# Cross attention by single heads, a narrow gate projection and layer norm's steps spread in a two-block transformer kernel

## The chip, the core and the metric

The kernel runs on one core of a Trainium2 chip. The core has five engines with instruction queues of their own: TensorE (PE, matmul), VectorE (DVE), ScalarE (ACT), GpSimd (POOL) and SyncE (SP), which here only starts DMA transfers. They meet through semaphores. The metric is the device time of one execution in microseconds; less is better.

## What is computed

Two transformer blocks in sequence over 256 tokens of width 2048, in float32. The three places of the change lie in this part of the reference (shortened):

```python
# first block, convolution branch
u = causal_depthwise_conv(u, w_dw[l], b_dw[l])
u = jax.nn.silu(layernorm(u, g_conv_ln[l], b_conv_ln[l]))      # u: 256 x 1024
o_cv = jnp.einsum('bsc,cd->bsd', u, w_conv_out[l])

# second block, gates of the DeltaNet group: 8 heads, 16 of the columns of p = u @ w_in
qkv, z, ga, gb = jnp.split(p, [3 * DN_WIDTH, 4 * DN_WIDTH, 4 * DN_WIDTH + DN_HEADS], axis=-1)
beta = jax.nn.sigmoid(gb)
g = -jnp.exp(a_log) * jax.nn.softplus(ga + dt_bias)

# second block, cross attention: 4 heads of 128, 256 memory tokens
q = (hn @ wq).reshape(b, s, XA_HEADS, XA_HEAD_DIM)
scores = jnp.einsum('bshd,bmhd->bhsm', q, k).astype(jnp.float32) * (XA_HEAD_DIM ** -0.5)
probs = jax.nn.softmax(scores, axis=-1).astype(v.dtype)
o = jnp.einsum('bhsm,bmhd->bshd', probs, v).reshape(b, s, XA_WIDTH)
return o @ wo
```

## The kernel before

**Weights and activations.** Activations lie transposed in SBUF: features on the 128 partitions, 256 tokens in the free dimension. Every float32 operand of a large product is kept as two rounded parts, hi and lo, with hi + lo = value. A product is hi x hi, hi x lo and lo x hi. Weights come in slabs of 512 x 256 elements (128 partitions x 4 k-tiles x 256 columns, 512 KB). There are four buffers each of `raw`, `hi` and `lo`. For a slab SP loads `raw`, ACT rounds it to `hi` (L324), DVE subtracts (`lo`, L364), and the PE runs 8 hi matmuls over 512 columns (activation hi and lo side by side, L481) and 8 lo matmuls over 256 columns (L488). `raw` of slab s+4 is loaded once `lo` of slab s is written; `hi` of slab s+4 is written once the PE has used slab s.

**Gemm.** A `Gemm` is one weight matrix. Its blocks of 256 output columns are two tiles `t` of 128 columns each, one PSUM bank each (`pg[:, par, t]`, two parities). After a block, ACT copies the second half of the sums to `half` (`take_half`, L336), and DVE adds the first half and stores (`evacuate`). In every engine's program the splits of block v+1 stand ahead of the evacuation of block v, and `follows=` names the Gemm whose first block is split ahead of the last evacuation. The order of the program is written out by hand: `after(m)` is called behind block m's evacuation, and `each()` behind every slab (PE) or every split (ACT, DVE); generators with `yield` put a stage's small steps there.

**Layer norm (`ln_act`, `ln_dve`, `ln_pe`).** It is called as `after(m)` of `g_sbo`, which has 8 blocks of 2 slabs. At m = 2 the deviation is computed and the normed values `conv_y` written (L1031). At m = 3 ACT makes 8 sigmoids of 256 columns (L1016). At m = 4 DVE makes 8 affine steps in place (L1036), then their product with the sigmoids over 2048 columns (L1039). At m = 5 and 6 the product is rounded and split. Behind `ln_act` ACT has two sigmoids of gates (L1052) for the attention's gate branches.

**Gates.** `g_gab` has one block of four slabs. Its 16 wanted columns are the first 16 of 256. With `apart=DN_H` (8) the second tile starts at column 8, so that the 8 columns of `gb` arrive on partitions 0 to 7 too; each tile is still 128 columns wide. Ahead of it runs `g_dn`, behind it `g_vz`. `gates_act` and `gates_dve` are the first steps of `dn_core`, and they begin with the first split of `g_vz`'s second block (its fifth slab). The DVE begins with L1418 and the ACT chain runs from L1398 to L1403 with its table loads; only behind it stands the split of the sixth slab. During `g_gab`, DVE has the convolution steps L1295 of the last block of `g_dn`.

**Cross attention.** `g_xq` makes the queries in two blocks (heads 0 and 1, then 2 and 3). Scores lie in `all4`, 8 slices of 256 columns in 4 banks. Its first half (q = 0, heads 0 and 1) runs beside `g_xq` (`xat_beside_*`); the rest is `xat_pe`, `xat_act`, `xat_dve`. A half is: scores, maximum (L2318), 4 exponentials with sums (L2292), division (L2325), 8 transposes (L2239), copy to `xp` (L2330), outputs (L2247), hi (L2298) and lo (L2334). `begin_xo_pe` starts the output projection `g_xo` with heads 0 and 1 (its first two k-tiles, L2272 and L2277), and the generic code runs the other two (`begun=2`).

## Time and profile before

| what | us |
|---|---|
| median of 3 runs | 2841.81 (2840.72 to 2848.27) |
| the profiled execution, its own time | 2841.37 |
| span of its trace | 2839.6 |
| PE busy in the span | 2778.5 |
| DVE busy | 1945.3 |
| ACT busy | 1418.9 |

The span goes from the first to the last instruction; the profiled execution took 1.8 us more around it. Busy times of engines overlap. The granted clock is the share of TensorE's full speed (2.4 GHz) that was allowed; 0.50 is the lower level of 1.2 GHz. A row's bracket tells how long the engine stood still before it, and what ended that.

### The profile page before, as it was taken

What the parts mean: (1) busy time and instruction counts of PE and PEld (TensorE: products, weight loads), DVE (VectorE), ACT (ScalarE), POOL (GpSimd) and SP (SyncE); (2) the same over time, 40 slices, a digit from 0 to 9 for tenths busy, and PEclk for the clock granted to TensorE, in tenths of its full rate; (3) what the DMA queues carried; (4) which work ended last, traced back from release to release, by engine and by line L of the source; (5) the groups of instructions that cost most, each with busy time, mean ns of one, the idle gap of its engine ahead of it and who ended that gap; (6) DMA issues with size and microseconds to landing.
All of it is one profiled execution on the core that took longest, in us unless ns stands there. A gap on an engine that the chain in (4) does not pass through costs nothing.

```text
span 2839.6 us, 48075 instructions
## 1 busy us (share of the span) xinstructions
PE 2778.5 (98%) x18522; PEld 2402.3 (85%) x18522; DVE 1945.3 (69%) x2356; ACT 1418.9 (50%) x1815; POOL 118.7 (4%) x130
## 2 busy tenths in 40 slices
PE   9999999999999999999999999989989999999998
PEld 8888888888888888888887888788878888888886
DVE  7888887778656556565777676955867556565664
ACT  6545557566434344344666446544654444343444
POOL 0000000150000000000000000131200000000000
PEclk9999999999999999999999999999999999999999
DMA  7555544766566665656564444402646666666664
GB/s 245 182 185 171 178 157 153 231 189 200 186 195 190 192 190 184 198 184 196 146 193 138 131 123 124 134 4 83 192 134 186 195 186 195 194 185 193 191 189 152
DMA packets 415244, 487.90 MB, mean 172 GB/s; under 512 B 14961, under 2 KB 346737, under 8 KB 415073
## 3 DMA queue, kind: packets, MB, share of 16 engines
q1 hardware_dynamic: 413216, 478.55, 54.6%
q0 software_dynamic: 1856, 6.98, 0.7%
q8 instruction: 118, 1.93, 0.3%
q14 instruction: 54, 0.43, 0.1%
HBM read 482.33 MB, written 3.15 MB: 171 GB/s over the span
## 4 chain that ended last, share of the span: by engine, by line
PE 86%; DVE 7%; ACT 4%; issue 2%; DMA 0%; ACTq 0%; DVEq 0%; SPq 0%
PE pg L481 36%; PE pg L488 19%; PE pg L449 16%; PE pg L454 8%; DVE lo L364 2%; PE p L1178 1%; DVE work L891 1%; ACT hi L324 1%; PE p L1195 1%; DVE xa L749 1%; PE p L1625 0%; DVE work L869 0%; PE pg L1900 0%; PE p L1371 0%; PE p L1173 0%
## 5 line engine op out<-in xcount | busy, mean ns | idle before, releaser
L364 DVE TENSOR_TENSOR lo<-raw,hi 128x1024 fp32r<-128x1024 f32 x895 | 1085.1, 1231 | 692.4 <-ACT hi L324 689.0
L324 ACT ACTIVATE hi<-raw 128x1024 fp32r<-128x1024 f32 x894 | 938.1, 1058 | 1120.6 <-PE pg L488 653.7
L481 PE MATMUL pg<-xa,hi 128*128 128x512 f32 x4224 | 1069.4, 395 | 2.6 <-DVE work L402 1.1
L481 PEld LDWEIGHTS pg<-xa,hi 128*128 128x128 f32 x4224 | 761.1, 189 | 144.2 <-issue 1.8
L488 PEld LDWEIGHTS pg<-xa,lo 128*128 128x128 f32 x4224 | 575.3, 190 | 50.1 <-DVE lo L364 9.4
L488 PE MATMUL pg<-xa,lo 128*128 128x256 f32 x4224 | 589.8, 282 | 4.5 <-DVE lo L364 4.5
L449 PE MATMUL pg<-hi,xb 128*128 128x512 f32 x2048 | 506.0, 389 | 0.0
L449 PEld LDWEIGHTS pg<-hi,xb 128*128 128x128 f32 x2048 | 383.9, 188 | 79.4
L454 PE MATMUL pg<-lo,xb 128*128 128x512 f32 x1024 | 273.7, 389 | 0.0
L481 PE MATMUL pg<-xb,hi 128*128 128x512 f32 x956 | 241.5, 394 | 4.4 <-ACT hi L324 2.9
L454 PEld LDWEIGHTS pg<-lo,xb 128*128 128x128 f32 x1024 | 192.2, 188 | 39.9
L481 PEld LDWEIGHTS pg<-xb,hi 128*128 128x128 f32 x956 | 172.4, 189 | 37.0 <-issue 3.2
L488 PEld LDWEIGHTS pg<-xb,lo 128*128 128x128 f32 x956 | 130.4, 190 | 11.9 <-DVE lo L364 2.5
L488 PE MATMUL pg<-xb,lo 128*128 128x256 f32 x956 | 133.4, 282 | 2.1 <-DVE lo L364 2.1
L336 ACT ACTIVATE half<-pg 128x512 f32<-128x512 f32 x156 | 91.4, 586 | 68.4 <-PE pg L488 68.4
L891 DVE SCALAR_TENSOR_TENSOR work<-u,vec,work 128x256 f32<-128x256 f32 x240 | 116.2, 484 | 7.7
L1258 DVE TENSOR_TENSOR rw_xx<-rw_xx,p 128x512 f32<-128x512 f32 x40 | 25.9, 684 | 35.1 <-PE p L1198 35.0
L425 DVE TENSOR_TENSOR xb<-sq,xb 128x512 f32 (+1 forms) x64 | 44.3, 693 | 6.4 <-DVE xb L422 0.9
L393 DVE TENSOR_TENSOR half<-pg,half 128x512 f32<-128x512 f32 x40 | 27.5, 688 | 26.8 <-ACT half L336 26.3
L416 DVE SCALAR_TENSOR_TENSOR sq<-sq,rs 128x512 f32<-128x512 f32 x64 | 44.3, 692 | 2.2
L420 DVE TENSOR_TENSOR sq<-sq 128x512 f32<-128x512 f32 x64 | 44.3, 692 | 2.2
L413 DVE TENSOR_TENSOR sq<-pg,half 128x512 f32<-128x512 f32 x64 | 43.8, 684 | 0.2 <-ACT half L336 0.2
(434 smaller groups left out, 1763.8 us busy)
## 6 DMA issues: line engine op xcount, KB each, us to landing
raw<-w_in SPq DMA_DIRECT2D x264, 512.0 KB, 4.4
raw<-ffn_w SPq DMA_DIRECT2D x256, 512.0 KB, 3.9
raw<-w_up SPq DMA_DIRECT2D x128, 512.0 KB, 3.9
raw<-w_down SPq DMA_DIRECT2D x128, 512.0 KB, 4.5
raw<-w_o SPq DMA_DIRECT2D x32, 512.0 KB, 4.8
raw<-w_out SPq DMA_DIRECT2D x32, 512.0 KB, 4.6
raw<-w_sb_out SPq DMA_DIRECT2D x16, 512.0 KB, 4.6
raw<-w_conv_out SPq DMA_DIRECT2D x16, 512.0 KB, 4.7
```

The lines of the kernel that those rows point to most:

```text
L324: nc.scalar.activation(hi[:, slot], raw[:, slot], ACT.Copy).then_inc(hi_ready, 1)
L336: nc.scalar.activation(half[:, :, :], pg[:, par, :, T:2 * T], ACT.Copy).then_inc(half_out, 1)
L364: nc.vector.tensor_tensor(lo[:, slot], raw[:, slot], hi[:, slot].bitcast(F32), ALU.subtract).then_inc(lo_ready, 1)
L413: nc.vector.tensor_tensor(sq[:, :, :], psum, half[:, :, :], ALU.add).then_inc(summed, 1)
L416: nc.vector.scalar_tensor_tensor(out=sq[:, :, :], in0=sq[:, :, :], scalar=0.0, in1=rs[:, None, :].to_broadcast([P, 2, T]), op0=ALU.max, op ...
L420: nc.vector.tensor_tensor(sq[:, :, :], sq[:, :, :], sq[:, :, :], ALU.mult).then_inc(squared, 1)
L425: nc.vector.tensor_tensor(rest, sq[:, :, :], place.bitcast(F32), ALU.subtract).then_inc(evacuated, 1)
L449: nc.tensor.matmul(pg[:, par, t, :], lhsT=g.x[:, j * g.kg + k, c:c + P], rhs=wide(hi[:, slot])[:, k], start=(first and k == 0 and part == ...
L454: ins = nc.tensor.matmul(pg[:, par, t, :], lhsT=g.x[:, j * g.kg + k, t * P:(t + 1) * P], rhs=wide(lo[:, slot])[:, k], start=False, stop=(l ...
L481: nc.tensor.matmul(pg[:, par, t, :], lhsT=hi[:, slot, k, c:c + P], rhs=g.x[:, kk, :], start=(j == 0 and k == 0), stop=False)
L488: ins = nc.tensor.matmul(pg[:, par, t, 0:T], lhsT=lo[:, slot, k, c:c + P], rhs=g.x[:, kk, 0:T], start=False, stop=(j == g.groups - 1 and k ...
L891: ins = nc.vector.scalar_tensor_tensor(out=acc, in0=x, scalar=v1("w_dw", 8 * j + c), in1=acc, op0=ALU.mult, op1=ALU.add)
```

## The change

It has three parts. **Gates:** `Gemm` takes `tiles` in place of `apart`, and `g_gab` has `tiles=1`: one tile of 128 columns, with splits and evacuation over 128 columns, and `ga` and `gb` on 16 partitions. ACT's sigmoid writes `gb` from `ga`, and DVE waits for it before it adds to `ga` in place; a transpose turns 16 rows, and a copy picks 8 of them. **Layer norm:** four sigmoids at m = 3 and four at m = 4; the affine steps at m = 3, into free tiles (`ln_affine`); the product at m = 4. **Cross attention:** from division to lo, every step is made for one head, `xo_psum(h)` gives heads h and h+1 different banks, and the steps are in another order.

```diff
-        self.k0, self.x_from, self.bias, self.apart, self.norm = k0, x_from, bias, apart, norm
+        self.k0, self.x_from, self.bias, self.tiles, self.norm = k0, x_from, bias, tiles, norm
...
-                nc.scalar.activation(hi[:, slot], raw[:, slot], ACT.Copy).then_inc(hi_ready, 1)
+                nc.scalar.activation(hi[:, slot, :, 0:g.tiles * P], raw[:, slot, :, 0:g.tiles * P], ACT.Copy).then_inc(hi_ready, 1)
...
-                    for t in range(2):
-                        c = t * g.apart
-                        for k in range(k0, KG):
+                    for k, t in [(k, t) for k in range(k0, KG) for t in range(2)] if k0 else []:
+                        if not t:
+                            XA_.dve.wait(pe, f"lo{k}")
+                        nc.tensor.matmul(pg[:, par, t, :], lhsT=hi[:, slot, k, t * P:(t + 1) * P], rhs=g.x[:, k, :],
+                                         start=False, stop=False)
+                    for t in range(0 if k0 else g.tiles):
+                        c = t * P
+                        for k in range(KG):
...
-            if m == 3:
+            if m in (3, 4):
                 act.wait_ge(ln_y, 1)
-                for c in range(8):
+                for c in range(4 * (m - 3), 4 * (m - 2)):
...
+            if m == 3:
+                dve.wait_ge(ln_y, 1)
+                for c in range(8):
+                    ins = nc.vector.tensor_scalar(work[:, TK + c, PAD:COLS], work[:, TY + c, PAD:COLS],
+                                                  v1("g_conv_ln", c), v1("b_conv_ln", c), ALU.mult, ALU.add)
+                ins.then_inc(ln_z, 1)
             if m == 4:
...
+                dve.wait_ge(ln_sig, 2)
+                dve.wait_ge(ln_z, 1)
+                nc.vector.tensor_tensor(conv_y, ln_affine, ln_tmp, ALU.mult).then_inc(ln_f, 1)
...
-        g_gab = Gemm(plan, "gab", w2in, D, 4096, BW, xa, "normed", (work, GA, PAD), apart=DN_H, norm=4)
+        g_gab = Gemm(plan, "gab", w2in, D, 4096, BW, xa, "normed", (work, GA, PAD), tiles=1, norm=4)
...
-            GT.act.done(nc.scalar.activation(gb, gb, ACT.Sigmoid), "beta")
+            GT.act.done(nc.scalar.activation(gb, ga, ACT.Sigmoid), "beta")
...
+            GT.act.wait(dve, "beta")
             GT.dve.done(nc.vector.tensor_scalar(ga, ga, al[:, 1:2], None, ALU.add), "dt")
...
-        xo_psum = lambda q: pg[:, 1, q].rearrange("p (h t) -> p h t", h=2)
+        xo_psum = lambda h: pg[:, 1, h % 2, h // 2 * T:h // 2 * T + T]
...
-            XA_.dve.wait(pe, "lo0")
+            XA_.dve.wait(pe, "lo1")
...
         def xat_pe(pe):
             turn_pe(pe, 0)
+            turn_pe(pe, 1)
             XA_.act.wait(pe, "v")
             scores_pe(pe, 1)
             outputs_pe(pe, 0)
+            outputs_pe(pe, 1)
             begin_xo_pe(pe)
-            turn_pe(pe, 1)
-            outputs_pe(pe, 1)
...
+            turn_pe(pe, 2)
+            outputs_pe(pe, 2)
+            turn_pe(pe, 3)
+            outputs_pe(pe, 3)
...
         def xat_act(act):
-            xat_exp(act, 1)
-            xat_hi(act, 0)
-            xat_hi(act, 1)
+            for h in (0, 1):
+                xat_hi(act, h)
+            for h in (2, 3):
+                xat_exp(act, h)
+            for h in (2, 3):
+                xat_hi(act, h)
...
         def xat_dve(dve):
-            xat_turned(dve, 0)
+            for h in (0, 1):
+                xat_turned(dve, h)
             xat_max(dve, 1)
-            xat_lo(dve, 0)
-            xat_div(dve, 1)
-            xat_turned(dve, 1)
-            xat_lo(dve, 1)
+            for h in (0, 1):
+                xat_lo(dve, h)
+            for h in (2, 3):
+                xat_div(dve, h)
+                xat_turned(dve, h)
+            for h in (2, 3):
+                xat_lo(dve, h)
...
-            XA_.dve.wait(pe, "lo1")
             gemm_pe(pe, g_xo, each=lambda: None, begun=2)
```

The order of instructions on DVE in `g_sbo`, blocks 3 to 5, before (L393 and L395 are a block's evacuation, L1036 and L1039 layer norm's steps):

```order
L364 TENSOR_TENSOR lo<-raw,hi 128x1024 x2
L393 TENSOR_TENSOR half<-pg,half 128x512
L395 TENSOR_TENSOR work<-work,half 128x2x256
L1036 TENSOR_SCALAR work<-work,vec 128x256 x8
L1039 TENSOR_TENSOR work<-work 128x8x256
```

And in the changed kernel, where the lines are called L394, L396, L1043 and L1049:

```order
L394 TENSOR_TENSOR half<-pg,half 128x512
L396 TENSOR_TENSOR work<-work,half 128x2x256
L1043 TENSOR_SCALAR work<-work,vec 128x256 x8
L365 TENSOR_TENSOR lo<-raw,hi 128x1024 x2
L394 TENSOR_TENSOR half<-pg,half 128x512
L396 TENSOR_TENSOR work<-work,half 128x2x256
L1049 TENSOR_TENSOR work<-work 128x8x256
```

The eight affine steps moved one block forward, ahead of a pair of lo splits; the product stayed.

On the PE in cross attention before, from the first transposes (L2239) over scores (L2223), outputs (L2247) and the projection's beginning (L2272, L2277) to its rest (L481):

```order
L2239 MATMUL p<-cst,xs 128x128 x8
L2223 MATMUL p<-work 128x256 x4
L2247 MATMUL pg<-xp,xv 128x256 x4
L2272 MATMUL pg<-xb,hi 128x512 x4
L2277 MATMUL pg<-xb,lo 128x256 x4
L2239 MATMUL p<-cst,xs 128x128 x8
L2247 MATMUL pg<-xp,xv 128x256 x4
L481 MATMUL pg<-xb,hi 128x512 x4
```

And in the changed kernel (transposes L2252, scores L2237, outputs L2259, beginning L2283 and L2288, rest L482):

```order
L2252 MATMUL p<-cst,xs 128x128 x8
L2237 MATMUL p<-work 128x256 x4
L2259 MATMUL pg<-xp,xv 128x256 x4
L2283 MATMUL pg<-xb,hi 128x512 x4
L2288 MATMUL pg<-xb,lo 128x256 x4
L2252 MATMUL p<-cst,xs 128x128 x4
L2259 MATMUL pg<-xp,xv 128x256 x2
L2252 MATMUL p<-cst,xs 128x128 x4
L2259 MATMUL pg<-xp,xv 128x256 x2
L482 MATMUL pg<-xb,hi 128x512 x4
```

The PE's order is the same up to the projection's beginning; behind it, transposes and outputs alternate by head. What moved ahead of that beginning is ACT's and DVE's work: their hi and lo of heads 0 and 1 now stand ahead of the exponentials and divisions of heads 2 and 3.

## Rows read from the trace of the kernel before

**Rows 1.** The page, its head and part 1: busy us (share of span) xinstructions.
```profile
span 2839.6 us, 48075 instructions
...
PE 2778.5 (98%) x18522; PEld 2402.3 (85%) x18522; DVE 1945.3 (69%) x2356; ACT 1418.9 (50%) x1815; POOL 118.7 (4%) x130
```

**Rows 2.** The page, part 5: group xcount | busy, mean ns | idle before, releaser.
```profile
L364 DVE TENSOR_TENSOR lo<-raw,hi 128x1024 fp32r<-128x1024 f32 x895 | 1085.1, 1231 | 692.4 <-ACT hi L324 689.0
L324 ACT ACTIVATE hi<-raw 128x1024 fp32r<-128x1024 f32 x894 | 938.1, 1058 | 1120.6 <-PE pg L488 653.7
```

**Rows 3.** Timeline around g_gab: start us, us, engine, line, operation, [idle before <-releaser].
```profile
1436.19 2.03 PE L481 MATMUL pg<-xa,hi 128*128 128x512 f32 x8
...
1439.00 2.02 PE L481 MATMUL pg<-xa,hi 128*128 128x512 f32 x8
...
1441.08 2.71 DVE L1295 SCALAR_TENSOR_TENSOR dnc<-work,vec,dnc 128x256 f32<-128x256 f32 x6 [0.38 <-ACT dnc L1310]
...
1450.48 1.06 ACT L324 ACTIVATE hi<-raw 128x1024 fp32r<-128x1024 f32 x1 [0.74 <-PE pg L488]
...
1453.18 0.34 DVE L1418 TENSOR_SCALAR work<-work,small 8x256 f32<-8x256 f32 x1
...
1458.73 0.20 ACT L1403 ACTIVATE small<-small 8x1 f32<-8x1 f32 x1
...
1461.39 2.00 PE L481 MATMUL pg<-xa,hi 128*128 128x512 f32 x8
```

**Rows 4.** DMA issues, 1425 to 1475 us: count, size, median us to landing.
```profile
raw<-w_in SPq DMA_DIRECT2D x19, 512.0 KB, 4.8
```

**Rows 5.** Timeline in g_sbo, where layer norm's steps lie.
```profile
466.58 4.03 ACT L1016 ACTIVATE work<-work,vec 128x256 f32<-128x256 f32 x8
...
468.34 0.69 DVE L395 TENSOR_TENSOR work<-work,half 128x512 f32<-128x512 f32 x1
...
472.74 2.09 PE L481 MATMUL pg<-xb,hi 128*128 128x512 f32 x8 [1.53 <-ACT hi L324]
...
474.96 2.00 ACT L324 ACTIVATE hi<-raw 128x1024 fp32r<-128x1024 f32 x2
...
476.30 2.67 DVE L1036 TENSOR_SCALAR work<-work,vec 128x256 f32<-128x256 f32 x8
...
479.00 2.29 DVE L1039 TENSOR_TENSOR work<-work 128x2048 f32<-128x2048 f32 x1
...
482.49 1.21 PE L488 MATMUL pg<-xb,lo 128*128 128x256 f32 x8 [2.08 <-DVE lo L364]
```

**Rows 6.** Timeline in cross attention.
```profile
2075.85 1.04 PE L2239 MATMUL p<-cst,xs 128*128 128x128 f32 x8
...
2078.25 1.97 PE L2223 MATMUL p<-work 128*128 128x256 f32 x8 [1.35 <-DVE work L409]
...
2080.05 1.89 PE L2247 MATMUL pg<-xp,xv 128*128 128x256 f32 x8
2080.25 1.23 DVE L2318 TENSOR_REDUCE small<-p 128x4 f32<-128x1024 f32 x1 [1.01 <-PE p L2223]
...
2083.52 0.61 ACT L2298 ACTIVATE xb<-pg 128x512 fp32r<-128x512 f32 x1
2084.17 0.69 DVE L2334 TENSOR_TENSOR xb<-pg,xb 128x512 fp32r<-128x512 f32 x1 [2.49 <-ACT xb L2298]
...
2084.91 1.86 PE L2272 MATMUL pg<-xb,hi 128*128 128x512 f32 x4 [2.97 <-DVE xb L2334]
...
2087.42 1.62 PE L2239 MATMUL p<-cst,xs 128*128 128x128 f32 x8
2089.08 1.23 DVE L2330 COPY xp<-p 128x1024 f32<-128x1024 f32 x1 [2.88 <-PE p L2239]
...
2093.77 1.19 PE L481 MATMUL pg<-xb,hi 128*128 128x512 f32 x4 [1.41 <-DVE xb L2334]
```

**Rows 7.** Windows view: stretch, PE, PEld, DVE, ACT, POOL busy, granted clock, DMA share, GB/s.
```profile
2086.00:2088.00 2.00, 2.00 (x9) 1.81 (x9) 0.20 (x1) 0.00 (x0) 0.00 (x0) 0.50 0.00 0
```

More of the change, by code:

```diff
@@ L335, in take_half @@
             if g.bias is None:
-                nc.scalar.activation(half[:, :, :], pg[:, par, :, T:2 * T], ACT.Copy).then_inc(half_out, 1)
+                nc.scalar.activation(half[:, 0:g.tiles, :], pg[:, par, 0:g.tiles, T:2 * T], ACT.Copy).then_inc(half_out, 1)
             else:
@@ L385, in evacuate @@
             dve.wait_ge(half_out, g.h0 + t + 1)
-            psum = pg[:, par, :, 0:T]
-            place = into[:, bass.ds(tile + 2 * t, 2), off:off + T]
+            psum = pg[:, par, 0:g.tiles, 0:T]
+            place = into[:, bass.ds(tile + 2 * t, g.tiles), off:off + T]
             if g.kind == "store":
@@ L483, in block @@
                     pe.wait_ge(lo_ready, s + 1 + RING)
-                    for t in range(2):
-                        c = t * g.apart
+                    for t in range(g.tiles):
+                        c = t * P
                         for k in range(k0, KG):
```

111 lines of the change are left out of this document (55 added, 56 removed).

## The prediction

> **What bounds the kernel now.** I read the page first, then the waits of TensorE and the timeline around the three places that the change touches. TensorE (PE) is busy 98% of a span of 2839.6 us [rows 1]. The reader is to see there that only two things can shorten this kernel: fewer matmuls, or fewer moments at which the PE stands still. Everything that ScalarE (ACT) and VectorE (DVE) do is free as long as a weight slab's two splits are ready when the PE comes to it. A slab of 8 hi and 8 lo matmuls takes 1439.00 - 1436.19 = 2.81 us of PE time [rows 3]; its splits cost 1.06 us on ACT (L324) and 1.23 us on DVE (L364) [rows 2]. So in the plain GEMM stretches both helpers have slack. Where a stage hangs other work on them, they can run out of it, and the change is about three such places. Nothing that the rows show outside them is altered, and what follows a place moves earlier as a block, so the effects add.
>
> **Part 1, the narrow gate projection (g_gab).** Before, its four slabs run both 128-column tiles; the second overlaps the first and serves only to bring rows 8 to 15 of the same product to partition 0. The change drops that tile: 4 slabs x 4 k-tiles x (1 hi + 1 lo) = 32 matmuls. Half of four slabs of 2.81 us is **5.6 us** off the PE. The weight transfer stays as wide. Splits and evacuation of this GEMM get narrower, I take 0.5 us less for each of four splits on ACT and DVE (half of 1.06 and of 1.23, less a fixed part).
>
> But this time was also the lead in which the helpers prepared the next GEMM, g_vz, whose first four splits are done while g_gab runs. I follow that chain. The PE starts g_gab at 1436.19 [rows 3] and would be done at 1436.19 + 5.6 = 1441.8. DVE runs six convolution steps (L1295), now 1441.08 to 1443.79 [rows 3]. They stand behind one narrow split on each engine in turn (0.5 us less on ACT, then 0.5 less on DVE), so I let them start 0.9 us earlier and end at 1442.9. Only then comes the lo split of g_vz's first slab, ending at 1444.1. The PE wants it about 1.85 us into the slab (its hi matmuls, 8 x 512 columns of 8 x 768), at 1441.8 + 1.85 = 1443.65: a wait of 0.45. The other three splits follow at 1.23 us each against 2.81 us of PE time, so they are in time.
>
> The second give-back is longer in coming. The raw buffer of g_vz's fifth slab (there are four) is released by that same lo split at 1444.1, and a load takes 4.8 us to land [rows 4]: 1448.95. Now ACT's hi split of it starts at 1450.48, released by the PE, so the load is hidden today; afterwards the load is what comes last. Hi ends at 1450.0, lo at 1451.25, and then DVE starts the gates (L1418), which it does at 1453.18 now. Thus the gates come only 1.9 us earlier, where the PE comes 5.2 us earlier. ACT's chain of gate functions with its table loads ends at 1458.93 now [rows 3], that is 5.75 us after L1418 starts; ACT is in order, so the sixth slab's hi split stands behind it and would end at 1451.25 + 5.75 + 1.06 = 1458.05 (it ends at 1459.98 now). The PE wants the sixth slab at 1461.39 - 5.6 + 0.45 = 1456.25. That is a wait of 1.8 us; today that split is ready 1.4 us ahead. The new wait for "beta" on DVE costs nothing: ACT's sigmoid is issued before DVE's lo split ends. Wider gate tiles (16 rows for 8) change no duration that matters, as all partitions work at once. Part 1: 5.6 - 0.45 - 1.8 = **3.35 us**. Bounds: 5.6 if the load lands early enough, 1.4 if the gates do not come earlier at all.
>
> **Part 2, layer norm beside g_sbo.** Two PE waits stand here: 1.53 us at 472.74 for ACT's hi split and 2.08 us at 482.49 for DVE's lo split [rows 5]. The first comes from eight sigmoids in one lot (L1016, 4.03 us). With four of them moved to the next step, the hi split ends 2.0 us earlier, at 470.7 for 472.7, and the PE wants it at 472.74 - 1.53 = 471.21. That wait goes. The other four follow one block later, where ACT starts 2 us earlier than now and so ends its first split as now, at 474.96 + 1.0 = 476.0; the PE wants block 6 at 482.49 - 2.08 - 1.85 - 1.53 = 477.0. It fits.
>
> The second comes from eight affine steps (L1036, 2.67 us) and a wide product (L1039, 2.29 us) in one step on DVE. The affine steps move one block ahead, into a hole: DVE ends L395 at 469.03 and then waits for ACT's late split. They run 469.0 to 471.7, the lo splits of block 5 (2 x 1.23) to 474.15, the evacuation (2 x 0.69) to 475.55, the product to 477.85, the lo split of block 6 to 479.1. The PE reaches that point at 482.49 - 2.08 - 1.53 = 478.9. 0.2 us of wait are left. The affine steps cost no wait of their own: block 5's first lo split ends at 472.9, the PE wants it at 471.2 + 1.85 = 473.05, a cover of only 0.15 us. Part 2: 3.61 - 0.2 = **3.4 us**. Bounds: 3.6, and 1.5 if the tight fits on both engines each miss by a microsecond.
>
> **Part 3, cross attention by single heads.** Now the second half of the softmax stands between the first outputs and everything else [rows 6]: outputs of heads 0 and 1 are done at 2080.05 + 1.89 = 2081.94, but ACT runs four exponentials first (its copy L2298 comes at 2083.52), DVE's L2334 follows, and the PE starts the output projection at 2084.91 after 2.97 us of nothing. With the copies ahead of the exponentials, and one bank for each head, so that ACT reads head 0 while the PE writes head 1: two-head copies of 0.61 and 0.69 us become single ones of about 0.39 and 0.42 (half of the step from 1024 to 512 columns taken off once more). DVE's maximum (L2318, and a tiny instruction that I take at 0.2, as I do below for each reciprocal) holds DVE until 2081.7 in any case. Hi of head 1 at 2082.35, lo at 2082.9: the PE starts **2.0 us earlier**, and is done with it in 1.4 us (half a slab) at 2084.35.
>
> The four exponentials take 2083.52 - 2081.7 = 1.8 us now; in twos behind the copies they end at 2083.3 and 2084.2. Division of head 2 (0.2 + 0.69) to 2084.35, its four transposes (half of 1.04, from 2075.85) to 2084.95, DVE's copy (0.69) to 2085.7, outputs (half of 1.89) to 2086.7. DVE divides head 3 only behind that copy, to 2086.6; transposes to 2087.2, copy to 2087.95, outputs to 2089.05, ACT's hi to 2089.5, DVE's lo to 2089.95. The rest of the projection's first block started at 2093.77. It starts 3.8 us earlier, and its head 2 half (2 of 4 hi matmuls, 0.45 us) has by then run in the wait: 3.8 + 0.45 = **4.2 us**. The price of smaller pieces is in it: each 1024 columns on DVE become 2 x 0.69 for 1.23.
>
> The clock matters here. The granted clock is 0.50 from 2086 to 2088 [rows 7], the lower of the two levels (1.2 GHz), after the PE had stood still for 2.97 us. In that stretch the projection's beginning took 2087.42 - 2084.91 = 2.51 us where half a slab is 1.4, and eight transposes 1.62 where they took 1.04: 1.7 us lost. My 4.2 takes the upper level throughout, since the longest wait left is about 1.1 us, as short as the 1.35 at 2078.25, after which no transposes or matmuls slowed. The Trainium skill, "TensorE: Matmul & The Clock Gate", section "Why this matters for your kernels", says that mid-kernel drops come of idle gaps between bursts; by that rule the drop goes, as I take it, and without it Part 3 is worth 2.5. Bounds: 2.5 and 5.0.
>
> **The sum.** 3.35 + 3.4 + 4.2 = 10.95 us. The profiled execution took 2841.37 us, 1.8 around its span, and lies 0.4 under the median of 2841.81. 2841.37 - 10.95 = **2830.4 us**.
>
> **Rivals.**
> - *More is given back.* The low clock stays in cross attention (1.7), and the gates come no earlier than today (another 1.9). For it: several waits of about 1 us follow each other there, and one 4.8 us load sets the gates. Against: each alone is as likely as not. 2830.4 + 3.6 = 2834.0.
> - *Less is given back.* The load of g_vz's fifth slab lands early, or ACT passes it; the 1.8 goes, and so does the 0.2 of layer norm. 2828.4. Against: DVE's order is fixed, and the load can't start before the lo split.
> - *The narrow projection brings nothing.* The DeltaNet stage behind it is set by ACT and DVE and swallows all 3.35. 2833.8. Against: after the gates the PE's slabs follow at their own pace in the timeline, and ACT waits for the PE again.
> - *Slower.* The new wait before g_vz's sixth slab pulls the clock to its lower level while dense slabs follow. At that level a slab costs 2.8 us more; four slabs in a row eat the whole 10.95, and at five the kernel takes 2830.4 + 14 = 2844.4. Decisive is a PE wait of 3 us or more there, where I get 1.8. Against: in cross attention the low level cost 1.7 us in all, which is 3.4 us spent at it, though the waits around it were longer.
>
> **Chances.** Forecast 0.55; more given back 0.18; less given back 0.14; narrow projection for nothing 0.09; slower 0.04. A measurement of this kernel can tell about 0.3% (8.5 us) from no change, so the edge is at 2833.3. The forecast case lies below it with most of its own spread (2828 to 2833), the two smaller ones just above: faster 0.75, same 0.21, slower 0.04. For 8 in 10 the range goes from 2826.5 to 2835.
>
> **What would show it.** Right: 32 fewer PE matmuls from the lo and hi lines and g_gab in 5.6 us; a PE wait of 1 to 2 us before the sixth slab of g_vz, released by ACT, with ACT's fifth hi split released by a DMA; no wait over 0.3 us in g_sbo; begin of the output projection about 1.1 us after the outputs of head 1, and a granted clock of 1.00 through cross attention. Wrong: a clock of 0.50 there, a wait over 1 us in g_sbo, which would mean that the 0.15 us cover was not enough, or new waits on the DeltaNet stage's transposes and masks, which would mean that ACT and DVE do not catch up.

## The result and the profile after

| kernel | median us (lowest to highest) | runs |
|---|---|---|
| before | 2842.32 (2839.76 to 2848.27) | 6 |
| changed | 2826.58 (2824.51 to 2827.92) | 6 |

The ratio is 0.9943, with a 95% interval of 0.9932 to 0.9953: 15.7 us faster. The prediction said 2830.4, with a range down to 2826.5, and a gain of 10.95 us; against the medians measured side by side it fell short by almost 5 us. The three mechanisms that it named are all in the trace. Its sum lacked about 1 us in them. Most of the rest goes with a term that it had at one place only, stretches at the lower clock; by how much, and at which places, the runs show in part only.

Page of the changed kernel, head and part 1, beside [rows 1]:

```profile
span 2825.9 us, 48022 instructions
...
PE 2770.7 (98%) x18490; PEld 2394.9 (85%) x18490; DVE 1943.0 (69%) x2364; ACT 1416.1 (50%) x1817; POOL 116.7 (4%) x130
```

The 32 matmuls are gone (18522 to 18490). The span is 13.7 us shorter, but PE busy only 7.8: 5.6 of that is the dropped tile, and this profile also has two stretches of 3.4 us at the low clock fewer than that of before. Standing still less is the other half.

To say where the time went I compared two traces slab by slab: for every weight slab, the time at which the PE gives it back (worked from the semaphore events of both traces). In plain stretches the difference stays constant to 0.1 us and it steps where something changed. From before to changed it steps so:

| place | forecast | step in the profiles |
|---|---|---|
| layer norm beside g_sbo, two waits | -3.4 | -1.75, -2.12 = **-3.9** |
| g_gab, four slabs of half the matmuls | -5.6 | 4 x -1.40 = **-5.6** |
| wait for g_vz's first lo split | +0.45 | **+0.46** |
| wait for g_vz's sixth slab | +1.8 | **+0.78** |
| a later wait for the gates on DVE | none | **+0.36** |
| cross attention | -4.2 | **-4.0** |
| a stretch at low clock at 1573, missing in the changed kernel's profile | none | -1.56 |

The first six lines add up to 11.9 us, where the prediction had 10.95. Of the 4.0 in cross attention, 1.6 is a stretch at the low clock that this profile of before has at 2085 (E6 below).

**Layer norm.** Timeline of the changed kernel in g_sbo (start us, us, engine, line, operation, [idle before <-releaser]), against [rows 5]:

```profile
466.54 2.06 ACT L1023 ACTIVATE work<-work,vec 128x256 f32<-128x256 f32 x4
...
468.92 2.67 DVE L1043 TENSOR_SCALAR work<-work,vec 128x256 f32<-128x256 f32 x8
...
472.86 1.13 PE L495 MATMUL pg<-xb,lo 128*128 128x256 f32 x8
...
475.11 2.28 DVE L1049 TENSOR_TENSOR work<-work 128x2048 f32<-128x2048 f32 x1
...
477.31 2.35 DVE L365 TENSOR_TENSOR lo<-raw,hi 128x1024 fp32r<-128x1024 f32 x2
...
478.58 1.22 PE L495 MATMUL pg<-xb,lo 128*128 128x256 f32 x8
```

No PE row has a bracket. The affine steps sit in the hole as laid out (468.92; the forecast said 469.0), and block 5's lo products begin at 472.86, without a wait: the cover of 0.15 us held. Block 6's lo split starts at 477.31, and its products at 478.58 wait for less than a view shows, where I had 0.2.

**The gate projection.** Timeline around g_gab, against [rows 3]. Everything here stands 3.9 us earlier because of the layer norm; g_gab's PE work starts at 1432.28 for 1436.19.

```profile
1432.28 1.09 PE L488 MATMUL pg<-xa,hi 128*128 128x512 f32 x4
...
1437.90 2.00 PE L488 MATMUL pg<-xa,hi 128*128 128x512 f32 x8
...
1440.11 1.21 PE L495 MATMUL pg<-xa,lo 128*128 128x256 f32 x8 [0.21 <-DVE lo L365]
...
1443.93 1.06 ACT L324 ACTIVATE hi<-raw 128x1024 fp32r<-128x1024 f32 x1 [3.18 <-DMA raw<-w_in]
...
1446.24 0.33 DVE L1429 TENSOR_SCALAR work<-work,small 16x256 f32<-16x256 f32 x1
...
1451.79 0.20 ACT L1413 ACTIVATE small<-small 16x1 f32<-16x1 f32 x1
...
1452.99 2.11 PE L488 MATMUL pg<-xa,hi 128*128 128x512 f32 x8 [0.51 <-ACT hi L324]
...
1464.82 0.18 DVE L1438 COPY small<-p 128x32 f32<-128x32 f32 x1
...
1465.05 0.30 PEld L1462 LDWEIGHTS p<-small,cst 128*128 128x128 f32 x2 [0.28 <-DVE small L1438]
1465.05 0.40 PE L1462 MATMUL p<-small,cst 128*128 128x16 f32 x2
```

The four slabs take 5.62 us (1432.28 to 1437.90) where they took 11.2. ACT's fifth hi split is released by a DMA after 3.18 us of waiting, the sixth slab's products by ACT: the chain of the forecast, link by link. Only its size is smaller, 0.78 for 1.8. At the end stands a wait that I had not: DVE's copy L1438, on which L1462 and its weight load (PEld) hang, comes behind three lo splits.

**Cross attention.** Timeline, against [rows 6], and one line of the windows view (stretch, PE, PEld, DVE, ACT, POOL busy, granted clock, DMA share, GB/s), against [rows 7]:

```profile
2068.65 1.97 PE L2237 MATMUL p<-work 128*128 128x256 f32 x8 [1.36 <-DVE work L411]
...
2070.45 1.89 PE L2259 MATMUL pg<-xp,xv 128*128 128x256 f32 x8
...
2071.51 0.38 ACT L2313 ACTIVATE xb<-pg 128x256 fp32r<-128x256 f32 x1 [4.46 <-PE pg L2259]
...
2072.79 0.42 DVE L2353 TENSOR_TENSOR xb<-pg,xb 128x256 fp32r<-128x256 f32 x1 [0.39 <-ACT xb L2313]
...
2073.27 1.20 PE L2283 MATMUL pg<-xb,hi 128*128 128x512 f32 x4 [0.93 <-DVE xb L2353]
...
2074.78 0.60 PE L2252 MATMUL p<-cst,xs 128*128 128x128 f32 x4
...
2076.16 1.13 PE L2259 MATMUL pg<-xp,xv 128*128 128x256 f32 x4 [0.78 <-DVE xp L2349]
...
2079.29 0.80 PE L482 MATMUL pg<-xb,hi 128*128 128x512 f32 x2
...
2080.57 0.74 PE L482 MATMUL pg<-xb,hi 128*128 128x512 f32 x2 [0.48 <-DVE xb L2353]
```

```profile
2074.00:2076.00 2.00, 1.38 (x11) 1.05 (x9) 1.18 (x2) 0.58 (x4) 0.00 (x0) 1.00 0.00 0
```

From the start of the outputs to the start of the projection it was 2084.91 - 2080.05 = 4.86 us and is now 2073.27 - 2070.45 = 2.82: 2.04 earlier, where I had 2.0. ACT reads head 0 at 2071.51, while the PE still writes head 1 in another bank until 2072.34. The longest wait left inside is 1.36 us, the one wait of 2.97 is 0.93, 0.78, 0.78 and 0.48, and in this profile the clock is at its upper level from 2058 to the end of the stage. That does not hold for every execution. In five of the seven profiles that have the stage in its new form (E3, E7, E10, E12 and E15, not this one and E4; E9 and E13 alter it) a stretch at 0.50 begins between 2057.9 and 2069.7, at the wait of about 1.9 us ahead of the stage's first scores (L2237), which the change leaves as it was; it costs 1.7 to 1.9 us in the steps.

### The profile page after: what moved, and what is told of

Same layout as the page of the kernel before. It is cut to its first block, busy times and chain, and to the rows that moved or that the text cites. A ratio compares the mean times of both kernels' runs of the same rounds, so it can differ in the third digit from the quotient of the medians.

```text
span 2825.9 us, 48022 instructions
## 1 busy us (share of the span) xinstructions
PE 2770.7 (98%) x18490; PEld 2394.9 (85%) x18490; DVE 1943.0 (69%) x2364; ACT 1416.1 (50%) x1817; POOL 116.7 (4%) x130
## 4 chain that ended last, share of the span: by engine, by line
PE 85%; DVE 8%; ACT 4%; issue 2%; DMA 1%; ACTq 0%; DVEq 0%; SPq 0%
PE pg L488 35%; PE pg L495 19%; PE pg L451 16%; PE pg L456 8%; DVE lo L365 2%; PE p L1188 1%; DVE work L898 1%; ACT hi L324 1%; DVE xa L756 1%; PE p L1205 1%; PE p L1638 0%; DVE work L876 0%; PE pg L1913 0%; DVE dnc L1305 0%; PE p L1381 0%
## 5 line engine op out<-in xcount | busy, mean ns | idle before, releaser
L324 ACT ACTIVATE hi<-raw 128x1024 fp32r<-128x1024 f32 (+1 forms) x894 | 935.5, 1056 | 1117.9 <-PE pg L495 652.3
L336 ACT ACTIVATE half<-pg 128x512 f32<-128x512 f32 (+1 forms) x156 | 91.1, 584 | 66.1 <-PE pg L495 66.1
L394 DVE TENSOR_TENSOR half<-pg,half 128x512 f32<-128x512 f32 x40 | 27.5, 689 | 26.1 <-ACT half L336 25.6
```

The source lines that it names most:

```text
L324: nc.scalar.activation(hi[:, slot, :, 0:g.tiles * P], raw[:, slot, :, 0:g.tiles * P], ACT.Copy).then_inc(hi_ready, 1)
L336: nc.scalar.activation(half[:, 0:g.tiles, :], pg[:, par, 0:g.tiles, T:2 * T], ACT.Copy).then_inc(half_out, 1)
```

## Experiments

All comparisons are with runs of the kernel before on the same chip. "Step" is a step of the slab-by-slab comparison.

### E1, E2, E3: each part alone. E4: the changed kernel again

Each is the kernel before with the lines of the diff that belong to one part:

```diff
 E1 -g_gab = Gemm(..., xa, "normed", (work, GA, PAD), apart=DN_H, norm=4)
    +g_gab = Gemm(..., xa, "normed", (work, GA, PAD), tiles=1, norm=4)     (and the gates on 16 partitions)
 E2 -            if m == 3:
    +            if m in (3, 4):                                           (and affine steps at m == 3)
 E3 -            xat_exp(act, 1)
    +            for h in (0, 1):
    +                xat_hi(act, h)                                        (and every step by one head)
```

> The kernel before with the narrow gate projection alone; layer norm and cross attention as before. Theory A (the parts are independent, and what the whole change gained beyond the forecast comes from TensorE's low-clock stretches in the DeltaNet stage, which fall where they fall): about 4.1 us less than before in the profiled slab times (5.6 off g_gab, 0.5 and 1.1 given back), and the low stretch behind the gates may stay or go. Rival B (the narrow projection itself takes that stretch away): 5.7 us, with the stretch near 1575 us gone. Rival C (the parts help each other): under 3 us.

> The kernel before with layer norm's steps spread alone. Theory A: 3.9 us less up to the end of g_sbo, both waits there gone, and nothing given back later; the low-clock stretches of the DeltaNet stage may fall otherwise, plus or minus 1.6. Rival B: exactly 3.9, with the stretch near 1575 us in its place. Rival C: under 3.

> The kernel before with cross attention by single heads alone. Theory A and B: 4.0 us less, a granted clock of 1.00 through cross attention, everything ahead of it as before. Rival C: 2.5 or less, with the low clock still there.

> The changed kernel once more, unaltered. Theory A: the sum of the three alone within 1.5 us, 12 to 15 us less than before; the number of low-clock stretches in the DeltaNet stage differs from the first profile of it or stays, by chance. Rival B: the same stretches at the same places as in its first profile. Rival C: more than the sum of the three by 3 us or more.

| | median us | ratio to before (2841.62), 95% interval | steps of the part |
|---|---|---|---|
| E1 gates | 2836.73 | 0.9982 (0.9973 to 0.9991) | -5.61 +0.45 +0.75 +0.36 = -4.05 |
| E2 layer norm | 2836.48 | 0.9978 (0.9969 to 0.9987) | -1.76 -2.13 = -3.89 |
| E3 cross attention | 2837.23 | 0.9983 (0.9974 to 0.9992) | -4.05 |
| E4 all | 2827.26 | 0.9947 (0.9933 to 0.9961) | -4.04, -3.90, -4.03 |

The parts don't interact: each makes alone the same steps as together, to 0.05 us, and the medians add (4.9 + 5.1 + 4.4 = 14.4, E4 measures 14.4). So the rival by which the DeltaNet stage swallows the narrow projection is out. But the steps add up to 12.0, and the medians to 14.4. In one job that is no more than a hint, since E4's interval reaches from 11.1 to 19.0 us. Something that has to do with the clock is there to be seen: besides these steps the traces differ by single ones of 1.5 to 1.9 us, up or down, in places that the edit doesn't touch, and at each a stretch of 3.4 us with a granted clock of 0.50 begins in one trace and not in the other (times and lengths from the clock records of the traces). E3's profile has such a stretch at 2069.7, so the clock of 1.00 through cross attention that was expected of it did not come, though its step of -4.05 did.

### E5, E6: the order alone, and the clock alone, in cross attention

E5 keeps pairs of heads and only puts ACT's copy ahead. E6 keeps everything and gives the PE 12 idle matmuls, whose results nobody reads, in the wait of 2.97 us.

```diff
 E5         def xat_act(act):
+            xat_hi(act, 0)
             xat_exp(act, 1)
-            xat_hi(act, 0)
             xat_hi(act, 1)
 E6         def begin_xo_pe(pe):
+            for _ in range(12):
+                nc.tensor.matmul(pg[:, g_xo.b0 % 2, 0, :], lhsT=hi[:, slot, 0, 0:P], rhs=xa[:, 0, :], start=True, stop=True)
             XA_.dve.wait(pe, "lo0")
```

> The kernel before with one edit in cross attention: ACT's copy of heads 0 and 1 stands ahead of the four exponentials of heads 2 and 3; all pieces stay two heads wide. Theory D (the order is worth more than the single heads): the output projection begins 2.0 us earlier and its rest 2.3 us earlier, against 4.05 for the whole part; so single heads bring 1.75. Rival E (the pieces in single heads bring it): under 1 us, as the delayed exponentials give it back. With the low clock of the kernel before gone as well, up to 1.6 us more.

> The kernel before with one edit: 12 matmuls of 512 columns, whose sums are overwritten, run on TensorE while it waits for DVE ahead of the output projection's beginning, so that it is not idle there. Theory F (the low clock after that wait costs about 1.6 us of the 4.05): no low-clock stretch near 2085 us, and the slabs after cross attention 1.6 us earlier than before. Rival G (that stretch is hidden behind ACT and DVE): no change, within 0.3.

E5: 2841.76 us, ratio 0.9999 (0.9990 to 1.0008); step -2.04. E6: 2840.82 us, 0.9990 (0.9980 to 0.9999); step -1.60. Timeline of E5, then of E6 with one line of its windows view:

```profile
2079.62 1.89 PE L2247 MATMUL pg<-xp,xv 128*128 128x256 f32 x8
2082.92 1.20 PE L2272 MATMUL pg<-xb,hi 128*128 128x512 f32 x4 [1.41 <-DVE xb L2334]
...
2091.30 1.19 PE L481 MATMUL pg<-xb,hi 128*128 128x512 f32 x4 [1.41 <-DVE xb L2334]
```

```profile
2083.59 3.10 PE L2270 MATMUL pg<-xa,hi 128*128 128x512 f32 x12
2086.91 1.20 PE L2274 MATMUL pg<-xb,hi 128*128 128x512 f32 x4 [0.22 <-DVE xb L2336]
...
2088.42 1.03 PE L2239 MATMUL p<-cst,xs 128*128 128x128 f32 x8
```

```profile
2086.00:2088.00 2.00, 1.78 (x9) 1.14 (x8) 1.80 (x3) 0.13 (x1) 0.00 (x0) 1.00 0.00 0
```

E6 leaves the softmax as slow as it was and still gains 1.6 us in its profile: with the PE kept at work the clock is 1.00, the beginning of the projection takes 88.42 - 86.91 = 1.51 us for 2.51, and the eight transposes 1.03 for 1.62 [rows 6]. That is 1.6 us where the prediction had put 1.7 down to the low clock. One profile could be luck, and in E8, E11 and E14 the unfilled wait of 2.97 us is followed by a clock of 1.00 as well; but each of these three had a stretch from 2065 to 2070, just ahead of it. The three profiles with this wait unfilled and no such stretch ahead (before, E1, E2) all drop behind it, and E6, which has none ahead either, does not. E5 then says what the order is worth in pairs: 2.04, of which 1.6 is the clock and only 0.4 the order. The rest of Part 3, some 2 us, needs the single heads. As a median, E5 can't be told from before, and E6 only just.

### E7: the gates one split later. E8: the sigmoids alone

E7 is the changed kernel, with the gates' first step behind the sixth split and not the fifth, and the later ones as they were. E8 is the kernel before with the eight sigmoids in two fours; the affine steps stay.

```diff
 E7         def gates_act(act):            (and the same in gates_dve)
+            yield
             blocks_out(act, g_gab)
 ...
-            yield from skip(9)
+            yield from skip(8)
 E8 -                for c in range(8):
+                for c in range(4 * (m - 3), 4 * (m - 2)):
 ...
-                dve.wait_ge(ln_sig, 1)
+                dve.wait_ge(ln_sig, 2)
```

> The changed kernel with the gates' first step on ACT and DVE one split later, so that the hi split of g_vz's sixth slab no longer stands behind ACT's gate chain. Theory H (that queue is what gives back 0.75 us): the wait ahead of the sixth slab goes, 0.75 us less; the 0.36 at the tenth stays. Rival I (the loads are what is late): the wait moves to the sixth slab's load or to the gates' transposes on TensorE, and the sum is 0.3 or less.

> The kernel before with only the eight sigmoids of layer norm in two lots of four; the affine steps stay at m = 4 ahead of the product. Theory J (each wait has its own engine and its own cause): the first wait (ACT, 1.76 us in the slab times) goes; the second (DVE, 2.13) grows by about as much as TensorE comes earlier less what DVE comes earlier, to 2.3; the sum is 1.6 us less than before. Rival K (both waits come from ACT): 3 us or more. Low-clock stretches may add or take 1.6 in this one profile.

E7: 2831.03 us, 0.9954 (0.9940 to 0.9967). Against the changed kernel its steps are -0.78, +0.81 and +1.10. Timeline of E7:

```profile
1464.28 1.22 PE L495 MATMUL pg<-xa,lo 128*128 128x256 f32 x8 [0.55 <-DVE lo L365]
1466.65 0.39 PE L1464 MATMUL p<-small,cst 128*128 128x16 f32 x2 [1.15 <-DVE small L1440]
```

The wait for the sixth slab goes, as Theory H had it, but two others come, and the sum is 1.1 us worse where it had 0.75 better. At this place in the order, then, the 0.78 can't be saved: ACT's table loads for the gates (three of 1.28 us) stand somewhere, and PE steps that hang on the gates come soon. Other places were not tried.

E8: 2838.97 us, 0.9991 (0.9982 to 1.0000); steps -1.77, -0.19, and one of +1.57 that is a low clock. Timeline of E8 and one line of its windows view:

```profile
480.53 1.22 PE L488 MATMUL pg<-xb,lo 128*128 128x256 f32 x8 [1.88 <-DVE lo L364]
481.59 3.53 PE L481 MATMUL pg<-xb,hi 128*128 128x512 f32 x8
```

```profile
482.00:484.00 2.00, 2.00 (x6) 1.58 (x5) 1.53 (x3) 2.00 (x3) 0.00 (x0) 0.50 0.86 278
```

Each wait of the layer norm has its own engine, as the prediction took it: the sigmoids cost the first, the affine steps the second, which shrinks by 0.19 where the expectation had it grow to 2.3. The new thing is the second line: 8 hi matmuls that take 2.00 us took 3.53, right behind a wait of 1.88.

### E9: the order undone under single heads

The changed kernel, but ACT makes the exponentials of heads 2 and 3 before it copies heads 0 and 1 out.

```diff
-            for h in (0, 1):
-                xat_hi(act, h)
             for h in (2, 3):
                 xat_exp(act, h)
-            for h in (2, 3):
+            for h in (0, 1, 2, 3):
                 xat_hi(act, h)
```

> The changed kernel with its single heads, but ACT makes the exponentials of heads 2 and 3 before it copies the outputs of heads 0 and 1 out (the order of before). E5 and E6 say that the order by itself is worth about 0.4 us at full clock and 2.0 us where it also takes the low clock away. Theory K (in the single-head version ACT's order is what lets the projection begin early): the copies of heads 0 and 1 come behind two exponentials of 1.4 us each, so the projection begins 2 to 2.8 us later than in the changed kernel; part of it comes back, since heads 2 and 3 are then turned with no wait. At the slab times the end of cross attention is 1 to 2.5 us later than in the changed kernel, and the low clock may be seen again behind the long wait. Rival L (banks of single heads alone do it): under 0.5 us later.

2833.47 us, 0.9965 (0.9952 to 0.9979); the changed kernel in the same job (E12) has 2829.18. The step is +5.4 where Theory K had 1 to 2.5. Timeline and one line of windows:

```profile
2075.57 1.20 PE L2283 MATMUL pg<-xb,hi 128*128 128x512 f32 x4 [2.82 <-DVE xb L2351]
...
2078.96 2.08 PE L2259 MATMUL pg<-xp,xv 128*128 128x256 f32 x4 [0.78 <-DVE xp L2347]
...
2084.19 2.71 PE L482 MATMUL pg<-xb,hi 128*128 128x512 f32 x4
```

```profile
2080.00:2082.00 2.00, 1.89 (x7) 1.20 (x5) 0.07 (x1) 0.38 (x1) 0.00 (x0) 0.50 0.00 0
```

The place was right: the projection begins 1.9 us later (6.51 us after the start of the scores L2237, for 4.62), behind a wait of 2.82. The size was not, since this execution (like each profile, one draw) stayed at 0.50 for 10.2 us behind that wait, over nearly all of the rest: outputs of one head took 2.08 for 1.13, the projection's hi matmuls 2.71 for 0.80 + 0.74. The medians are 4.3 us apart, more than the 2.5 of Theory K too. In this version, then, the order seems to be worth more than its own 2 us, because it keeps the longest wait short; the share of the clock in the 4.3 rests on this one profile.

### E10 to E15: fillers in the waits, and more profiles of both kernels

E11 is the kernel before, E12 and E15 are the changed kernel. E10 and E13 put idle matmuls into waits that the change left, E14 puts them into the layer norm's second wait of before.

```diff
 E10          for l in range(LEVELS):
+                if S is DN and l < 2:
+                    for _ in range(4):
+                        nc.tensor.matmul(ps[1][:, 0:T], lhsT=const("ident"), rhs=work[:, DK + 4 * r, PAD:COLS], start=True, stop=True)
 E13          for l in range(LEVELS):
+                for _ in range({0: 2}.get(l, 0) if S is DN and not r else 0):
+                    nc.tensor.matmul(ps[1][:, 0:T], lhsT=const("ones"), rhs=cst[:, 0:2], start=True, stop=True)
 ...
         def scores_pe(pe, q):
+            if not q:
+                warm(3)
 E14          behind a slab's hi matmuls, ahead of the wait for lo:
+                    if g is g_sbo and (i, v, j) == (3, 0, 0):
+                        for _ in range(7):
+                            nc.tensor.matmul(ps[3][:, :], lhsT=hi[:, slot, 0, 0:P], rhs=g.x[:, 0, :], start=True, stop=True)
```

> The changed kernel with four idle matmuls of 256 columns put before each of the first two steps of the triangular inverse in the DeltaNet stage, where TensorE waits 2.02 us (at 1548.29) and 1.81 us (at 1563.95) for VectorE; the matmuls' results are read by nobody. In nine of the ten profiles so far one to two stretches of half clock of 3.4 us, worth 1.55 to 1.8 us each in the slab times, begin near these waits, 1.2 on the mean. Theory M (a wait that is left without matmuls is what puts the clock at its low level by chance, so the fillers take it away): no stretch of half clock between 1545 and 1580, and 1 to 2.5 us less than the changed kernel in the medians (2824.3 to 2826). Rival N (the clock falls by chance that has nothing to do with these waits, or the fillers only add to the wait): one stretch or more is still there, or the slab times are later by over 0.5 us; median 2826.5 to 2829.

> The kernel before, again, for a second profile of it and as the size of what the timing can't tell: ratio 0.999 to 1.001. Its stretches of half clock are counted. If a stretch behind the layer norm's second wait (near 482) and one behind the cross attention's wait of 2.97 us come in most executions of it, this profile shows at least one of them; slab times otherwise within 0.3 us of the first profile.

> The changed kernel, again, beside e10 on the same chip: ratio to the kernel before 0.993 to 0.996. Its profile should show no stretch of half clock near 482 nor between 2060 and 2090, and one or two in the DeltaNet stage.

> The changed kernel with idle matmuls in two of the waits behind which its profiles show half clock: two of 256 columns (1.0 us) before the first step of DeltaNet's triangular inverse (wait of 2.02 us at 1548.29 for VectorE; E10's four began 0.94 us into it and ended 0.84 us too late, and its fillers of the later steps lay where nothing was waited for), and three (1.5 us) ahead of cross attention's first scores (wait of 1.88 us at 2057.98). Theory M' (fillers that fit keep the clock up): no half clock from 1545 to 1560 and none from 2057 to 2070, slab times otherwise as in the changed kernel within 0.2 us, median 1 to 2.5 us under the changed kernel's. Rival N' (the drops are drawn anew elsewhere, or are no fewer): a stretch is there or as many elsewhere, median within 0.8 us of the changed kernel's.

> The kernel before with seven idle matmuls of 512 columns (1.75 us) in the layer norm's second wait (2.08 us ahead of the lo products at 482.49). The wait is hardly shorter at its end, so the slab times without the clock stay as they are. In seven profiles of kernels that still have this wait, before twice, E1, E3, E5, E6 and E8, five show half clock right behind it (not the first of before, nor E5), worth 1.57 us at the slab times. Theory P (this stretch is what the layer norm's part gave beyond its 3.9 us): no half clock near 482, and a median 0.5 to 1.6 us under the kernel before (ratio 0.9994 to 0.9998, hardly to be told from 1). Rival Q (the excess is noise of the timing): half clock is there, or the median is the same or higher.

> The changed kernel once more, on the chip and in the rounds of E13, so that these two can be set against each other: ratio 0.993 to 0.996. One or two stretches of half clock near 1549, 1566 or 2060.

| | median us | ratio to before, 95% interval |
|---|---|---|
| E10 | 2834.48 | 0.9970 (0.9958 to 0.9982) |
| E11 before | 2842.08 | 0.9998 (0.9988 to 1.0008) |
| E12 changed | 2829.18 | 0.9949 (0.9936 to 0.9963) |
| E13 | 2827.51 | 0.9945 (0.9931 to 0.9959) |
| E14 | 2838.98 | 0.9990 (0.9981 to 1.0000) |
| E15 changed | 2827.85 | 0.9941 (0.9928 to 0.9955) |

**E11 and E14.** E11's profile has what the first profile of before had not, half clock right behind the layer norm's second wait. Timeline of E11 and a window of it, then the same place in E14:

```profile
482.58 1.89 PE L488 MATMUL pg<-xb,lo 128*128 128x256 f32 x8 [2.08 <-DVE lo L364]
...
484.27 2.92 PE L481 MATMUL pg<-xb,hi 128*128 128x512 f32 x8
```

```profile
484.00:486.00 2.00, 2.00 (x8) 1.61 (x7) 1.52 (x3) 2.00 (x3) 0.00 (x0) 0.50 0.89 266
```

```profile
480.11 1.75 PE L485 MATMUL p<-xb,hi 128*128 128x512 f32 x7
482.35 1.22 PE L491 MATMUL pg<-xb,lo 128*128 128x256 f32 x8 [0.49 <-DVE lo L364]
483.41 2.00 PE L481 MATMUL pg<-xb,hi 128*128 128x512 f32 x8
```

Of seven profiles of kernels with this wait (before, E1, E3, E5, E6, E8, E11) five show the stretch; of nine without it (changed, E2, E4, E7, E9, E10, E12, E13, E15) none does, and E14's, with the wait filled, doesn't either. A random draw would hardly sort itself so, and E8, in which the wait of 1.53 us ahead is gone, shows the stretch all the same. The drop costs about 1.6 us and comes in 5 of 7: 1.1 us a run on the mean that no step between the first two profiles could show. Theory P holds by its row; its median (3.7 us under before, the interval reaching from 0 to 5.4) agrees in sign and is too wide to size it.

**E10.** There is no stretch from 1545 to 1580, and still the kernel is 5.3 us slower than E12, where Theory M had it faster: the fillers were badly placed. Timeline of E10:

```profile
1547.21 1.99 PE L1178 MATMUL p<-work,cst 128*128 128x256 f32 x8 [0.93 <-ACT sq L1573]
1549.13 1.15 PE L1194 MATMUL p<-cst,dn_nm 64*64 64x64 f32 x32
...
1553.11 1.89 PE L1178 MATMUL p<-work,cst 128*128 128x256 f32 x8
```

A wait for ACT stands ahead of them that the longer one for DVE had hidden, so they end 0.84 us late; at the second level nothing had been waited for (1553.11), nor in the stage's second round, where each four cost 1.7 to 1.9 us more in the steps (slabs given back at 1652 and 1656). **E13** puts half as many at the one place and three ahead of the first scores. There is no half clock from 1545 to 1560 nor from 2057 to 2070, and the slab times stay, so the fillers fit. E12, of which no stretch from 2060 on was expected, has one from 2057.9 to 2061.3 and shows what they stand against. Timeline of E13, then E12's window right behind the same wait (which ended at 2057.97):

```profile
1547.03 1.13 PE L1177 MATMUL p<-cst 128*128 128x256 f32 x4 [0.95 <-ACT sq L1572]
...
2057.81 1.99 PE L2241 MATMUL p<-work 128*128 128x256 f32 x8 [0.61 <-DVE work L411]
```

```profile
2058.00:2060.00 2.00, 2.00 (x5) 1.64 (x6) 0.96 (x1) 0.00 (x0) 0.00 (x0) 0.50 0.66 232
```

But E13's profile has a stretch at 1562.7, at the next wait of 1.8 us, which has no filler, and its median is that of E15, 2827.51 and 2827.85. M' holds for the places, N' for the time. Whether fillers that fit gain anything here stays open, and no version beat the changed kernel.

**What the clock is worth in all.** Every run carries its mean granted clock. Over all runs of the two kernels beside the experiments, E4, E11, E12 and E15 among them, and the six runs of the changed kernel in the result:

| mean granted clock | before: mean us (runs) | changed: mean us (runs) |
|---|---|---|
| 0.993 | 2847.8 (7) | |
| 0.994 | 2845.3 (6) | |
| 0.995 | 2843.9 (30) | 2830.3 (2) |
| 0.996 | 2840.8 (42) | 2829.0 (5) |
| 0.997 | 2840.1 (6) | 2827.3 (7) |
| 0.998 | 2837.1 (5) | 2825.0 (6) |
| 0.999 | | 2822.3 (1) |
| all | 2842.3 (96) | 2827.1 (21) |

Within each kernel, the runs differ with the clock, by about 2 us for each 0.001. At the same mean clock the two are 12 to 14 us apart, over all runs 15.2 (give or take 1.1, twice the standard errors of 0.3 and 0.5). Since the low level is half of the upper, time at the low level is 2 x (1 - clock) x time: 25.5 us on the mean for before, 17.2 for the changed kernel, in both some 7 to 8.5 us of it at the very end, when the PE is done. The 8.3 us of difference cost, by the steps of 1.55 to 1.8 us for 3.4 us at it, about 4.1 us, and by the table (0.0014 of clock) about 3. The steps hold 1.6 of that already (cross attention), so 11.9 + 2.5 = 14.4 us is accounted for out of 15.2, or 13.3 by the table.

**Where it goes, the profiles show in part.** The difference of 8.3 us is 2.4 stretches a run. Behind the layer norm's second wait 0.7 of them go (5 in 7 profiles, then none in 9). In cross attention (2057 to 2090) the six profiles with both waits as in before (before, E1, E2, E8, E11, E14) have seven stretches (E1's of 6.8 us counted as two), and the seven with the new form five: 0.45 a run less, worth some 0.5 to 0.8 us and not the 1.6 of the first pair of profiles. In the DeltaNet stage (1545 to 1580) it is about one a profile with or without the narrow projection. The other half of the 2.4 shows at no place, and with one profile a run stays open.

## Why the prediction was right or wrong

**The bound** named two things that can shorten the kernel, fewer matmuls and fewer idle moments of the PE. Both moved the span as said; a third did too, time at the low clock (25.5 us a run before, 17.2 after), and the prediction had it at one place only.

**Part 1, 3.35 forecast, 4.0 measured.** The 5.6 and the 0.45 are exact. The term that failed is 1.8 for the sixth slab; it measured 0.78. The mechanism is the one described (DMA releases the fifth hi split, the gates follow, ACT's chain of 5.75 us from L1429 to the end of L1413, the sixth split behind it). What was mis-sized is the load. I took the median of 4.8 us [rows 4]; this one went out when the first lo split ended, near 1440.05, and had landed by 1443.93, 3.9 us. The DMA view of the changed kernel shows the queue around it (1425 to 1470 us in 40 slices of 1.125 us, busy share in tenths):

```profile
DMA  9960079999810049999998100008999700489999
```

Slices 13 and 14, 1438.5 to 1440.75, are at zero: the load started on idle DMA engines, while the median mixes in loads that queue behind each other. That idleness is the likely reason for its being short; no run tested it. Against that stands a term that I left out, +0.36 for DVE's copy behind three lo splits. E7 shows that the two waits hang together.

**Part 2, 3.4 forecast, 3.9 measured.** The affine steps began within 0.1 us of the plan, and E8 confirms one engine for each wait. The forecast's fault is the 0.2 us of wait left (there is none: block 6's lo split began at 477.31, 0.5 us before the 477.85 of the plan), and its ceiling of 3.6: a wait costs more than its bracket. The 1.53 came back as 1.75, since the group behind a wait also runs longer (2.09 us for 2.00); the last 0.1 I can't name.

**Part 3, 4.2 forecast, 4.0 measured.** Begin 2.04 earlier for 2.0; the clock's part 1.6 by E6 for 1.7. The clock at 1.00 through the stage came in the profiles of the changed kernel and of E4, and in five others not: a stretch began at the unchanged wait of 1.9 us instead, so that the close match of 4.0 with 4.2 is in part the luck of the two profiles compared. Over several executions Part 3 is nearer to 3, that is 2.4 of waits and the 0.5 to 0.8 above. On the low clock, the rule I cited from the Trainium skill ("TensorE: Matmul & The Clock Gate", "Why this matters for your kernels"), that drops in the middle of a kernel come of idle gaps between bursts, agrees in kind with E6: the same wait, with and without work in it, gave 1.00 and 0.50. Not every such wait was followed by a drop (E8, E11, E14), and drops came behind waits of 1.8 to 2.1 us too.

**The sum** failed in what it left out: of the clock it had 1.7 us at one place, where the runs' mean clocks give 3 to 4.1 us. I read the low clock where the profile of before happened to show it next to an edit, and nowhere else. The step that failed is the second wait of the layer norm (2.08 us). It is of the same kind as the one of 2.97 us, and I costed it at its bracket alone, with nothing for the clock, because in that one execution nothing slowed behind it. In 5 of the 7 profiles with this wait something does, at 1.57 us each: 1.1 us. E2's median (5.1 us) agrees with 3.9 + 1.1, but its interval, 3.7 to 8.8, holds 3.9 as well. A forecast that had priced a chance of the drop at every such wait would have had 4.0 + 5.0 and about 3 for Part 3, some 12 us. From there to the 15.2 no place is shown.

**The rivals.** More given back: no. Less given back: near, in that the load did land early, by 1 us of the 1.8. Narrow projection for nothing: refuted by E1. Slower: the new wait is 0.5 us in the bracket, and no low clock stands near it in any profile of the change. Its condition, a wait of 3 us or more, was too high a bar: drops began behind waits of 1.8 us. **Chances.** Faster was right. The range had its lower end at 2826.5, 4 us under the forecast. The measured 2826.58 is only just inside it, and the measured ratio times the 2841.81 that the prediction started from is 2825.6, outside. The gain of 15.7 us is more than the upper bounds of the three parts together (5.6 + 3.6 + 5.0 = 14.2); a term that is in no one's bounds can't be covered that way.

**Open:** 0.8 to 1.9 of the 15.2 us, with its uncertainty of 1.1; at which places half of the time saved at the low clock is saved, and by what; which of the executions drop behind a wait, and why; and the stretches of 3.4 to 10.2 us between 1825 and 1950, in the RWKV stage, in every kernel here, which no experiment touched.

## What to carry to other kernels

A single profile shows one draw of the clock, in what goes and in what stays. Before summing an edit that removes a PE wait of some 2 us or more in front of dense matmuls, look at the mean granted clock of all runs and at more than one profile, and price the drop by its share. When two helpers' work stands in front of the PE, move the piece that the PE needs ahead of the piece that it doesn't, and split both so that neither queue holds it for long (here waits of 0.5 to 0.9 us were left); the gain is the wait and, in part of the executions, the clock. Fillers need the same care as real work: what is waited for ahead of them, and whether a loop runs them where nothing was waited for.

## What the runs showed that I had not expected

- The stretches at half clock in these traces lasted 3.4, 6.8 or 10.2 us, and 3.4 us of it cost 1.55 to 1.8 us in dense slabs. Outside the RWKV stage (1825 to 1950) they begin near the end of waits of 1.8 to 3.0 us, at 482, 1549 to 1573, 2058 to 2085, and not in every execution; none began behind the waits of 1.3 to 1.6 us in these places. Where a drop near 2069 had come, none followed at 2085 (E8, E11, E14), behind the wait of 2.97 us that had one in before, E1 and E2. So a change that shortens the second wait does not always take a stretch away.
- Nearly the same wait can be followed by low clock of different length: 3.4 us in before, 6.8 in E1 (both behind 2.97 us) and 10.2 us in E9 (behind 2.82).
- A load of 512 KB landed 3.9 us after its buffer came free, against a median of 4.8 in the same stretch of before.
- Identical kernels in four jobs gave ratios of 0.9941 to 0.9949, and before against itself 0.9998 (0.9988 to 1.0008): 0.1% can be told here with this many runs.
